# Who issues the weight loads: SyncE's queue or GpSimd's own, in a two-block transformer kernel

## The chip, the cores and the metric

The kernel runs on one core of one Trainium2 chip. The metric is the device time of one launch, in microseconds (us); lower is better. Everything is float32 in memory. The engines are TensorE (PE in the profile, its weight load PEld), VectorE (DVE), ScalarE (ACT), GpSimd (POOL) and SyncE (SP), which here computes nothing and only issues transfers.

## The reference

One sequence of 1024 tokens with 1024 features goes through two blocks.

```
first block:   mod = c @ w_ada + b_ada            -> shift, scale, gate (1024 each)
               h = rmsnorm(x) * (1 + scale) + shift
               proj = h @ w_in                    -> glu, z, q, k, v, gates
               y_conv = (silu(layernorm(conv31(glu))) * silu(z_conv)) @ w_conv_out
               y_att  = (3 groups of dilated window attention * silu(z_att)) @ w_att_out
               x = rmsnorm(x + gate * ((sig(g1) * y_conv + sig(g2) * y_att) @ w_o))
second block:  proj = rmsnorm(x) @ w_in2 + b      -> pool, q, k, v, gates
               merged = sig * (pooling @ w) + sig * (window attention @ w)
               x = x + rmsnorm(merged @ w_out2)
               x = x + rmsnorm(relu(rmsnorm(x) @ w_up)^2 @ w_down),  4096 hidden features
```

## The kernel before, in words

**Three products for one.** Each float32 operand of a large product is cut into a high half (rounded to TensorE's fast float32 form) and a low half (the rest). A product is then three passes: high by high, high by low, low by high. Activations are cut by ScalarE (`act_hi`) and VectorE (`act_lo`, line 1239). Weights are cut by GpSimd.

**Pieces, chunks, units.** The weights of the projections come in `PIECES` of 128 x 512 values (256 KB); eight make a chunk of 512 output columns. A piece is loaded into one of four buffers (`raw`, `RAW = 4`). GpSimd copies it to `w_hi` (line 870) and subtracts to get `w_lo` (line 872), in the helper `split_piece`; the semaphore `w_ready` counts the finished ones. `w_hi` and `w_lo` hold two chunks, so the cutting of chunk c begins (gate `acc_ready` in the loop over `PIECES`) when TensorE has ended chunk c - 2. TensorE works a chunk as units of 24 (or 12) matmuls into four PSUM banks. The names of the chunks that matter below: `q`, `k`, `v` of three attention groups; `za`, `zc` (gates); `yc`, `ya` (the two output projections of block one), `wo`; `pl`, `q3`, `kv3`, `g2p`, `g2a`, `yp`, `yb`, `w2` in block two; then 16 rounds of the MLP, each with four `up` and four `down` pieces.

**SyncE's order.** All transfers are issued by SyncE in one program order: `next_piece` (line 507) waits for `w_ready >= n - 3`, so that the buffer is free, and issues piece n; `prefetch(u)` calls it as the program passes unit u, between stores, activations' loads and other traffic. At the start SyncE issues x, the pieces of `w_ada` (`ada_piece`, line 537, eight buffers), stores four rows of `mod`, reads shift and scale back (lines 564 and 565), then calls `next_piece` eight times, and only then issues `w_ada` pieces 32 to 47, which are the `gate` rows. TensorE's program has all six `w_ada` rows (`ada_row_`, line 1777) ahead of the first projection. In the MLP SyncE's loop calls `mlp_pieces` (line 793).

**Stretches in which VectorE's work stands between two stretches of matmuls:**

- "h": affine (line 1291) and low half (line 1239) of the first activations.
- "Z": while `zc` is computed, each of eight token blocks is combined from three attention groups (lines 1429 to 1432), transposed, and loaded for the next (lines 669, 677).
- "uz": after `zc`, 8 rounds of lines 1456, 1457, 1459 and 1239 before `yc` can go on.
- "az", "mg" and "m2": low halves (line 1239) before `ya`, `wo` and `w2`.
- "q3": pooling (lines 1565 to 1570) and rotation in the `q3` chunk.
- "norm 2": lines 1502 to 1536 during `w2`, before the MLP.

Of the kernel before, what the change touches and what calls it, by code (L numbers as in the profile page):

```python
# [42 lines left out]
RAW = 4  # L43
# [134 lines left out]
def build(nc, A, out):  # L178

    chunks, units, items, U, chunk_last = plan()  # L180
# [9 lines left out]
    with ExitStack() as ctx:  # L190
# [213 lines left out]
        def unit_range(first, last):  # L404
            return units[U[first]:U[last] + 1]
# [87 lines left out]

        @block.sync
        def _(sp):
            piece = [0]

            def next_piece():

                n = piece[0]  # L500
                if n >= NP0:
                    return
                if n >= RAW:
                    sp.wait_ge(w_ready, n - RAW + 1)
                c, s = PIECES[n]
                for cols, src in piece_src(chunks[c], s):
                    sp.dma_start(raw[:, n % RAW, cols], src).then_inc(raw_ld[n % RAW], 16)
                piece[0] += 1

            def prefetch(u):  # L510

                if u in unit_chunk:
                    c, i = unit_chunk[u]
                    if i < 8 and piece[0] < 8 * (c + 1) + i + 1:
                        next_piece()

            def store_item(u, dst):
                wait_evac(sp, u)
                sp.dma_start(dst, slot(u)).then_inc(ev_st[E[u] % EVN], 16)
# [43 lines left out]
                sp.wait_ge(mod_st[n], v)  # L563
            sp.dma_start(c_sh, cols_of(mod_d[0, 0:D]), allow_slow_non_contiguous=True).then_inc(ada_col, 16)
            sp.dma_start(c_gs, cols_of(mod_d[0, D:2 * D]), allow_slow_non_contiguous=True).then_inc(ada_col, 16)
            for _ in range(8):
                next_piece()
            for p in range(32, 48):
                ada_piece(p)
            for n in (4, 5):  # L570
# [62 lines left out]
            def attention_io(g):  # L633
                per = att_share(len(ATT_STAGES[g]))
                us = att_units(g)
                for s in range(64):
                    for i in units_done(len(ATT_STAGES[g]), s):
                        u = us[i]
                        prefetch(u)
                        if i >= 1 and us[i - 1][0] in DST:  # L640
                            w = us[i - 1]
                            store_item(w, feature_tile(DST[w[0]], w[1], w[2]))
                        if i >= 1 and us[i - 1] == ("ua", 1, 1):
                            conv_load(0)
                            conv_load(1)
                    conv_io(("step", g, s))
                    if g < 3 and s >= 6 and (s - 6) % 4 == 1:
                        store_heads(g, s - 4)
                w = us[-1]
                store_item(w, feature_tile(DST[w[0]], w[1], w[2]))  # L650
                if g < 3:
                    store_heads(g, 63)
                    store_stats(g)

            def qkv_io(g):
                for u in STAGE_QKV[g]:
                    prefetch(u)
                    conv_io(u)

            for g in range(NG):  # L660
# [31 lines left out]
            attention_block(0)  # L692
            late = None
            for u in STAGE_Z:
                prefetch(u)
                if u[0] == "zc":
                    if late:
                        store_item(late, feature_tile(DST["zc"], late[1], late[2]))
                    late = u
                if u[0] == "lt" and u[2] == 1 and u[1] + 1 < NB:  # L700
                    conv_block(u[1] + 1)
                if u[0] == "at" and u[1] + 1 < NB:
                    attention_block(u[1] + 1)
# [20 lines left out]

            i = 0
            for u in units[U[("yc", 0, 0)]:U[("ya", 7, 1)] + 1]:
                prefetch(u)
                gate_load(i, ("uz", 7), u, "gc" if u[0] == "yc" else "ga")
                i += 1

# [11 lines left out]
            n = 0  # L742
            for h in range(2):
                for B in range(NB):
                    prefetch(("wo", B, h))
                    if n >= 2:
                        sp.wait_ge(n_x[0], n - 1)
                    sp.dma_start(xt2[n % 2], A["x"][0, P * B:P * B + P, HALF * h:HALF * h + HALF]
                                 ).then_inc(n_ld[0][n % 2], 16)
                    n += 1  # L750
                    if h and B >= 2:
                        sp.wait_ge(n_y[0], B - 1)
                        sp.dma_start(x1_d[P * (B - 2):P * (B - 1), :], tokT[:, B - 2, :]).then_inc(n_st[0], 16)
# [3 lines left out]


            b2 = A["b_in_2"]
            for u in unit_range(("pl", 0, 0), ("pl", 3, 1)):  # L760
                prefetch(u)
# [7 lines left out]
            for u in unit_range(("q", 3, 0), ("kt", 3, 7)):  # L769
                prefetch(u)  # L770
            for t in range(4):
                for h in range(2):
                    wait_evac(sp, ("pm", t, h))
# [7 lines left out]
                    for h in range(2):  # L781
                        wait_stored(sp, (n, t, h))
            for i, u in enumerate(unit_range(("yp", 0, 0), ("yb", 7, 1))):
                prefetch(u)
                gate_load(i + 32, ("y2", 3), u, "g2p" if u[0] == "yp" else "g2a")


            def mlp_pieces(src, j, before):

                for p in range(4):  # L790
                    sp.wait_ge(w_ready, before + p)
                    dst = raw[:, p, :].rearrange("p (k n) -> p k n", k=2) if src is up_src else raw[:, p, :]
                    sp.dma_start(dst, src(j, p)).then_inc(raw_ld[p], 16)
# [4 lines left out]
            sp.wait_ge(n_st[0], 16 * 8)  # L798
            for h in range(2):
                for B in range(NB):  # L800
                    prefetch(("w2", B, h))
                    if h:
                        if B >= 2:
                            sp.wait_ge(n_y[1], B - 1)
                        sp.dma_start(res[B % 2], x1_d[P * B:P * B + P, :]).then_inc(n_ld[1][B % 2], 16)
                        if B >= 2:
                            sp.dma_start(x2_d[P * (B - 2):P * (B - 1), :], tokT[:, B - 2, :]).then_inc(n_st[1], 16)
                        if B == 3:
                            mlp_pieces(up_src, 0, NP0 - 3)
            for B in (6, 7):  # L810
                sp.wait_ge(n_y[1], B + 1)
                sp.dma_start(x2_d[P * B:P * B + P, :], tokT[:, B, :]).then_inc(n_st[1], 16)


            with sp.Fori(1, NJ) as k:
                mlp_pieces(up_src, k, NP0 + 8 * k - 7)
                mlp_pieces(down_src, k - 1, NP0 + 8 * k - 3)
            mlp_pieces(down_src, NJ - 1, NP0 + 8 * NJ - 7)


            sp.wait_ge(n_xn[1], 8)
# [17 lines left out]
        def _(pool):  # L839
# [25 lines left out]

            pool.iota(posi[:, 24:32], pattern=[[P, 8]], base=0, channel_multiplier=1).then_inc(consts, 1)

            def split_piece(n, src, dhi, dlo):

                pool.tensor_copy(dhi, src).then_inc(w_hi_done, 1)  # L870
                pool.wait_ge(w_hi_done, n + 1)
                pool.tensor_tensor(dlo, src, dhi.bitcast(F32), ALU.subtract).then_inc(w_ready, 1)  # L872

            for n, (c, s) in enumerate(PIECES):
                pool.wait_ge(raw_ld[n % RAW], raw_total[n])
                if c >= 2 and s == 0:
                    pool.wait_ge(acc_ready, U[chunk_last[c - 2]] + 1)
                split_piece(n, raw[:, n % RAW, :], w_hi[:, c % 2, s, :], w_lo[:, c % 2, s, :])
                if chunks[c] == ("kv", 3) and s == 7:

                    pool.wait_ge(att_max, 64 * NG)
                    pool.affine_select(out=band[:, :], in_=band[:, :], compare_op=ALU.is_gt, fill=NEG, base=0,
                                       pattern=[[1, 2 * P]], channel_multiplier=-1).then_inc(consts, 1)

            def mlp_split(region, n0, ld, free):

                pool.wait_ge(acc_ready, free)
                for p in range(4):
                    pool.wait_ge(raw_ld[p], RAW_BASE[p] + 16 * (ld + 1))
                    pool.sem_inc(piece_seen)  # L890
                    split_piece(n0 + p, raw[:, p, :], w_hi[:, 0, region + p, :], w_lo[:, 0, region + p, :])


            last_chunk = len(chunks) - 1
            mlp_split(0, NP0, 0, U[chunk_last[last_chunk - 1]] + 1)
            mlp_split(4, NP0 + 4, 1, U[chunk_last[last_chunk - 1]] + 1)
            mlp_split(0, NP0 + 8, 2, M0 + 4)
            with pool.Fori(2, NJ) as k:

                mlp_split(4, NP0 + 8 * k - 4, 2 * k - 1, M0 + 20 * k - 32)  # L900
                mlp_split(0, NP0 + 8 * k, 2 * k, M0 + 20 * k - 16)
            mlp_split(4, NP0 + 8 * NJ - 4, 2 * NJ - 1, M0 + 20 * NJ - 32)

            for B in range(NB):
                pool.wait_ge(n_scaled, B + 1)
# [1068 lines left out]
```

## Time and profile before

| | |
|---|---|
| median of 3 runs | 2915.23 us (2912.63 to 2915.69) |
| profiled execution, its own time | 2915.05 us |
| its span, first to last instruction | 2912.9 us |
| mean granted TensorE clock | 0.971 of full |
| busy: TensorE, VectorE, GpSimd, ScalarE | 95%, 48%, 31%, 22% of the span |

The profile is one execution. A view lists either groups of instructions by source line, or the instructions in order of time (start, duration, engine, line, operation, output and input tile), with the idle time before one and what ended it in square brackets. "SPq" rows are issues by SyncE's queue; their duration is from the first to the last issue of the row. Two views give the waits: one by who waited for whom, one (the chain) that follows the work that ended last back to its start.

### The profile page before, as it was taken

The numbers are of one execution on the slowest core, as the hardware profiler recorded it, in microseconds if no ns is written. First come the engines' busy times: TensorE is split into PE (matmuls) and PEld (weight loads), VectorE is DVE, ScalarE is ACT, GpSimd is POOL, SyncE is SP. The second block draws the span as 40 slices with busy tenths as digits, with TensorE's granted clock in tenths as the row PEclk, the third lists the DMA queues.
The fourth block names the chain that finished last, engine by engine and source line by source line (L and its number), as shares of the span: only waits on it lengthen the run. The fifth ranks groups of instructions, "written<-read, shape, count | busy, mean of one in ns | idle before, by whom it ended". The sixth has DMA issues, their size and how long they took to land.

```text
span 2912.9 us, 33971 instructions
## 1 busy us (share of the span) xinstructions
PE 2759.7 (95%) x12436; PEld 2198.0 (75%) x12436; DVE 1386.1 (48%) x2569; ACT 627.4 (22%) x1495; POOL 897.2 (31%) x870
## 2 busy tenths in 40 slices
PE   6799999999999999877999989998999999999997
PEld 2487778987789877765778767776787888888886
DVE  1421245986667676564346432223545344344346
ACT  3212222112321122441014022222122101101102
POOL 0531122432224232222424322222323343343343
PEclk8899999999999999997999989999999999999999
DMA  5410111122212132453334122223422111111113
GB/s 174 131 51 26 57 55 58 56 66 75 84 54 73 49 98 84 158 165 122 100 111 148 30 67 65 59 65 127 130 94 98 44 50 50 43 51 50 43 54 126
DMA packets 155596, 236.10 MB, mean 81 GB/s; under 512 B 24764, under 2 KB 69564, under 8 KB 155464
## 3 DMA queue, kind: packets, MB, share of 16 engines
q1 hardware_dynamic: 155464, 234.35, 25.3%
q8 instruction: 82, 1.34, 0.2%
q14 instruction: 50, 0.41, 0.0%
HBM read 181.65 MB, written 52.64 MB: 80 GB/s over the span
## 4 chain that ended last, share of the span: by engine, by line
PE 87%; DVE 8%; DMA 3%; ACT 1%; issue 1%; POOL 0%; SPq 0%; POOLq 0%; ACTq 0%; DVEq 0%
PE ps L1748 50%; PE ps L1895 12%; PE ps L1927 11%; PE ps L1806 5%; PE ps L1816 3%; PE ps L1830 3%; PE ps L1760 2%; PE ps L1777 2%; DVE act_lo L1239 1%; DVE scr L1326 1%; DMA small<-st_d 1%; DMA scr<-in_x 1%; DVE scr L1429 0%; DVE big L1669 0%; DVE big L1519 0%
## 5 line engine op out<-in xcount | busy, mean ns | idle before, releaser
L870 POOL CAST w_hi<-raw 128x512 fp32r<-128x512 f32 x416 | 306.0, 736 | 1948.5 <-DMA raw<-in_w_in 938.3
L1748 PE MATMUL ps<-act_hi,w_hi 128*128 128x512 f32 x1344 | 557.6, 415 | 48.4 <-DVE act_lo L1239 46.2
L872 POOL TENSOR_TENSOR w_lo<-raw,w_hi 128x512 fp32r<-128x512 f32 x416 | 580.3, 1395 | 33.3
L1748 PE MATMUL ps<-act_lo,w_hi 128*128 128x512 f32 x1344 | 532.6, 396 | 0.0
L1748 PE MATMUL ps<-act_hi,w_lo 128*128 128x512 f32 x1344 | 530.2, 394 | 0.0
L1326 DVE SCALAR_TENSOR_TENSOR scr<-scr,small 128x512 f32<-128x512 f32 x480 | 421.0, 877 | 11.5
L1748 PE MATMUL ps<-w_hi,act_hi 128*128 128x512 f32 (+1 forms) x960 | 387.4, 404 | 6.8 <-DVE act_lo L1239 6.5
L1748 PE MATMUL ps<-w_hi,act_lo 128*128 128x512 f32 (+1 forms) x960 | 376.0, 392 | 0.0
L1748 PE MATMUL ps<-w_lo,act_hi 128*128 128x512 f32 (+1 forms) x960 | 375.8, 391 | 0.0
L1748 PEld LDWEIGHTS ps<-act_hi,w_hi 128*128 128x128 f32 x1344 | 256.4, 191 | 102.2 <-issue 54.3
L1748 PEld LDWEIGHTS ps<-act_lo,w_hi 128*128 128x128 f32 x1344 | 255.6, 190 | 57.6
L1748 PEld LDWEIGHTS ps<-act_hi,w_lo 128*128 128x128 f32 x1344 | 257.0, 191 | 45.7 <-issue 0.2
L1748 PEld LDWEIGHTS ps<-w_hi,act_hi 128*128 128x128 f32 x960 | 233.3, 243 | 31.8 <-issue 12.5
L1748 PEld LDWEIGHTS ps<-w_hi,act_lo 128*128 128x128 f32 x960 | 233.5, 243 | 21.0
L1748 PEld LDWEIGHTS ps<-w_lo,act_hi 128*128 128x128 f32 x960 | 234.4, 244 | 19.1
L1018 ACT ACTIVATE scr<-scr,stat 128x256 f32<-128x256 f32 (+1 forms) x256 | 118.6, 463 | 512.6 <-DVE stat L1349 511.2
L1681 DVE TENSOR_TENSOR big<-big,ps 128x512 f32<-128x512 f32 x224 | 150.0, 684 | 112.5 <-PE ps L1927 112.5
L1895 PE MATMUL ps<-act_hi,w_hi 128*128 128x512 f32 x512 | 200.1, 391 | 1.8 <-DVE act_lo L1536 1.8
L1895 PE MATMUL ps<-act_lo,w_hi 128*128 128x512 f32 x512 | 199.9, 390 | 0.0
L1895 PE MATMUL ps<-act_hi,w_lo 128*128 128x512 f32 x512 | 199.8, 390 | 0.0
L1927 PE MATMUL ps<-w_hi 128*128 128x512 f32 x512 | 199.3, 389 | 0.0
L1927 PE MATMUL ps<-w_lo,w_hi 128*128 128x512 f32 x512 | 199.2, 389 | 0.0
(173 smaller groups left out, 3113.5 us busy)
## 6 DMA issues: line engine op xcount, KB each, us to landing
raw<-in_w_in SPq DMA_DIRECT2D x176, 256.0 KB, 3.1
raw<-in_w_up SPq DMA_DIRECT2D x64, 256.0 KB, 2.7
raw<-in_w_down SPq DMA_DIRECT2D x64, 256.0 KB, 2.6
vreg<-in_w_ada SPq DMA_DIRECT2D x48, 256.0 KB, 3.5
raw<-in_w_in SPq DMA_DIRECT2D x72, 128.0 KB, 2.2
x_d<-big SPq DMA_DIRECT2D x16, 512.0 KB, 3.0
scr<-x_d SPq DMA_DIRECT2D x16, 512.0 KB, 4.2
o_d<-scr SPq DMA_DIRECT2D x48, 128.0 KB, 1.9
```

The costliest lines, as they stand in the source:

```text
L870: pool.tensor_copy(dhi, src).then_inc(w_hi_done, 1)
L872: pool.tensor_tensor(dlo, src, dhi.bitcast(F32), ALU.subtract).then_inc(w_ready, 1)
L1018: nc.scalar.activation(prob[a % 2][:, 0:n], prob[a % 2][:, 0:n], ACT.Exp, scale=-1.0, bias=stat[:, B, h:h + 1], accum_out=stat[:, B, 8 + h ...
L1326: nc.vector.scalar_tensor_tensor(ca, u_in[:, j:j + HALF], w[:, j:j + 1], ca, ALU.mult, ALU.add).then_inc(tap, 1)
L1681: ins = nc.vector.tensor_tensor(dst, dst, acc[i % ACC], ALU.add)
L1748: ins = nc.tensor.matmul(out_, lhs, rhs, start=(m == 0), stop=(m == 3 * nk - 1))
L1760: ins = nc.tensor.transpose(bank(u)[:, P * i:P * i + P], src, ident[:, :])
L1806: nc.tensor.matmul(ps_s[a % 2][:, 0:n], qT[rows, pair, P * B:P * B + P], keys, start=True, stop=True).then_inc(scores, 1)
L1816: ins = nc.tensor.transpose(ps_t[:, P * i:P * i + P], prob[a % 2][:, P * i:P * i + P], ident[:, :])
L1830: ins = nc.tensor.matmul(ps_o[:, 0:HD], probT[a % 2][:, P * i:P * i + P], v, start=(i == 0), stop=(i == n // P - 1))
L1895: ins = nc.tensor.matmul(out_, up_w[b][:, k, P * t:P * t + P], act_p[a][:, k, HALF * h:HALF * h + HALF], start=(m == 0), stop=(m == 23))
L1927: ins = nc.tensor.matmul(acc[i % ACC], hid[a][:, par, k, P * B:P * B + P], down_w[b][:, k, HALF * h:HALF * h + HALF], start=(m == 0), stop ...
```

## The change

GpSimd issues every weight piece itself. It starts the first four before its loop. After it has cut piece n it waits until its own low half is written (`w_ready >= n + 1`) and issues piece n + 4 into the buffer just read. The MLP's pieces follow in the same way from `mlp_split`, whose last argument says what to load. SyncE loses `next_piece`, `prefetch`, `mlp_pieces` and its MLP loop; all its other transfers stay in their order, with nothing between them.

```diff
@@ block.sync
-            def next_piece():
-                n = piece[0]
-                if n >= RAW:
-                    sp.wait_ge(w_ready, n - RAW + 1)
-                c, s = PIECES[n]
-                for cols, src in piece_src(chunks[c], s):
-                    sp.dma_start(raw[:, n % RAW, cols], src).then_inc(raw_ld[n % RAW], 16)
-            def prefetch(u): ...
@@ between the loads of shift and scale and w_ada pieces 32 to 47
-            for _ in range(8):
-                next_piece()
             for p in range(32, 48):
                 ada_piece(p)
...
-            with sp.Fori(1, NJ) as k:
-                mlp_pieces(up_src, k, NP0 + 8 * k - 7)
-                mlp_pieces(down_src, k - 1, NP0 + 8 * k - 3)
-            mlp_pieces(down_src, NJ - 1, NP0 + 8 * NJ - 7)
@@ block.gpsimd
+            def mlp_load(src, j, p):
+                dst = raw[:, p, :].rearrange("p (k n) -> p k n", k=2) if src is up_src else raw[:, p, :]
+                pool.dma_start(dst, src(j, p)).then_inc(raw_ld[p], 16)
+            def load_piece(n):
+                if n >= NP0:
+                    mlp_load(up_src, 0, n - NP0)
+                    return
+                c, s = PIECES[n]
+                for cols, src in piece_src(chunks[c], s):
+                    pool.dma_start(raw[:, n % RAW, cols], src).then_inc(raw_ld[n % RAW], 16)
             def split_piece(n, src, dhi, dlo):
                 pool.tensor_copy(dhi, src).then_inc(w_hi_done, 1)
                 pool.wait_ge(w_hi_done, n + 1)
                 pool.tensor_tensor(dlo, src, dhi.bitcast(F32), ALU.subtract).then_inc(w_ready, 1)
+                pool.wait_ge(w_ready, n + 1)
+            for n in range(RAW):
+                load_piece(n)
             for n, (c, s) in enumerate(PIECES):
                 pool.wait_ge(raw_ld[n % RAW], raw_total[n])
                 if c >= 2 and s == 0:
                     pool.wait_ge(acc_ready, U[chunk_last[c - 2]] + 1)
                 split_piece(n, raw[:, n % RAW, :], w_hi[:, c % 2, s, :], w_lo[:, c % 2, s, :])
+                load_piece(n + RAW)
...
-            def mlp_split(region, n0, ld, free):
+            def mlp_split(region, n0, ld, free, after):
                 pool.wait_ge(acc_ready, free)
                 for p in range(4):
                     pool.wait_ge(raw_ld[p], RAW_BASE[p] + 16 * (ld + 1))
                     pool.sem_inc(piece_seen)
                     split_piece(n0 + p, raw[:, p, :], w_hi[:, 0, region + p, :], w_lo[:, 0, region + p, :])
+                    if after:
+                        mlp_load(after[0], after[1], p)
...
-                mlp_split(4, NP0 + 8 * k - 4, 2 * k - 1, M0 + 20 * k - 32)
-                mlp_split(0, NP0 + 8 * k, 2 * k, M0 + 20 * k - 16)
+                mlp_split(4, NP0 + 8 * k - 4, 2 * k - 1, M0 + 20 * k - 32, (down_src, k - 1))
+                mlp_split(0, NP0 + 8 * k, 2 * k, M0 + 20 * k - 16, (up_src, k + 1))
```

## Rows read from the trace of the kernel before

**Rows 1.** The page's chain of work that ended last, by engine.

```profile
PE 87%; DVE 8%; DMA 3%; ACT 1%; issue 1%; POOL 0%; SPq 0%; POOLq 0%; ACTq 0%; DVEq 0%
```

**Rows 2.** TensorE's waits: total us, times, longest.

```profile
PE ps L1777 <- DMA vreg<-in_w_ada: 20.6, 1, 20.6
```

**Rows 3.** Order of time, SyncE's queue, 72 to 112 us: start, duration.

```profile
74.11 15.46 SPq L507 DMA_DIRECT2D raw<-in_w_in  x8
89.62 12.70 SPq L537 DMA_DIRECT2D vreg<-in_w_ada  x16
```

**Rows 4.** Order of time, TensorE, 75 to 112 us.

```profile
92.80 9.16 PE L1777 MATMUL ps<-vreg,small 128*1 128x512 f32 x16 [20.59 <-DMA vreg<-in_w_ada]
...
109.79 0.50 PE L1748 MATMUL ps<-w_hi,act_hi 128*128 128x512 f32 x1
```

**Rows 5.** Groups of VectorE by line, 76 to 101.6 us: busy us, mean ns.

```profile
L1239 DVE TENSOR_TENSOR act_lo<-big,act_hi 128x1024 fp32r<-128x1024 f32 x8 | 17.4, 2182 | 0.1
```

**Rows 6.** Order of time, VectorE, 0 to 62 us.

```profile
7.41 0.75 DVE L1245 TENSOR_SCALAR scr<-scr,small 128x1024 f32<-128x1024 f32 x1
```

**Rows 7.** Windows, first 12 us: busy, clock, DMA share, GB/s.

```profile
0.00:12.00 12.00, 3.63 (x16) 3.28 (x16) 1.84 (x4) 6.54 (x10) 3.80 (x29) 1.00 0.80 274
```

**Rows 8.** All instructions on the buffers `raw`: ns minimum, median, maximum.

```profile
L870 POOL CAST w_hi<-raw x416: 601/613/3265, 77.2 to 2860.1; 128x512 fp32r<-128x512 f32 x139
L872 POOL TENSOR_TENSOR w_lo<-raw,w_hi x416: 1261/1292/2152, 78.0 to 2860.8; 128x512 fp32r<-128x512 f32 x139
...
L793 SPq DMA_DIRECT2D raw<-in_w_down x64: 327/336/346, 2208.9 to 2839.7; - x64
```

**Rows 9.** Order of time, VectorE, "uz": first operation and last ones.

```profile
1305.36 0.81 DVE L1456 TENSOR_SCALAR big<-big,col 128x1024 f32<-128x1024 f32 x1 [7.25 <-ACT scr L1080]
...
1331.34 1.22 DVE L1457 SCALAR_TENSOR_TENSOR big<-scr,big 128x1024 f32<-128x1024 f32 x1
...
1334.88 1.10 DVE L1456 TENSOR_SCALAR big<-big,col 128x1024 f32<-128x1024 f32 x1
1336.01 2.18 DVE L1457 SCALAR_TENSOR_TENSOR big<-scr,big 128x1024 f32<-128x1024 f32 x1
```

**Rows 10.** Order of time, VectorE, "Z".

```profile
1190.60 1.90 DVE L1429 TENSOR_TENSOR scr<-scr,stat 128x512 f32<-128x512 f32 x3
...
1205.92 3.41 DVE L1429 TENSOR_TENSOR scr<-scr,stat 128x512 f32<-128x512 f32 x3
...
1295.93 1.28 DVE L1338 SCALAR_TENSOR_TENSOR scr<-scr,ps 128x512 f32<-128x512 f32 x2
```

**Rows 11.** Order of time, TensorE, "Z".

```profile
1211.88 1.50 PE L1760 MATMUL ps<-ident,scr 128*128 128x128 f32 x12 [1.12 <-DVE scr L1338]
...
1294.07 0.39 PE L1748 MATMUL ps<-act_lo,w_hi 128*128 128x512 f32 x1
```

**Rows 12.** Order of time, VectorE, "az" and "mg".

```profile
1427.73 7.36 DVE L1239 TENSOR_TENSOR act_lo<-vreg,act_hi 128x1024 fp32r<-128x1024 f32 x4 [0.40 <-ACT act_hi L922]
...
1479.93 9.16 DVE L1239 TENSOR_TENSOR act_lo<-big,act_hi 128x1024 fp32r<-128x1024 f32 x8
```

**Rows 13.** Order of time, GpSimd, the end of "m2".

```profile
2100.48 3.27 POOL L870 CAST w_hi<-raw 128x512 fp32r<-128x512 f32 x1 [33.47 <-DMA raw<-in_w_out]
```

**Rows 14.** Order of time, VectorE, "q3".

```profile
1669.14 0.69 DVE L1581 TENSOR_TENSOR scr<-ps,big 128x512 f32<-128x512 f32 x1 [3.06 <-PE ps L1748]
...
1689.25 0.17 DVE L1309 TENSOR_TENSOR scr<-scr 128x16 f32<-128x16 f32 x1
```

**Rows 15.** Order of time, VectorE, "norm 2": the same line two blocks apart.

```profile
2164.22 1.28 DVE L1514 SCALAR_TENSOR_TENSOR big<-big,stat,vreg 128x1024 f32<-128x1024 f32 x1
...
2179.58 1.28 DVE L1514 SCALAR_TENSOR_TENSOR big<-big,stat,vreg 128x1024 f32<-128x1024 f32 x1
...
2193.34 1.28 DVE L1514 SCALAR_TENSOR_TENSOR big<-big,stat,vreg 128x1024 f32<-128x1024 f32 x1
```

**Rows 16.** The chain in order of time, MLP: half of a round.

```profile
2331.08 21.76 PE ps L1927 x96
```

More of the change, by code:

```diff
@@ L495, in _ @@
         def _(sp):
-            piece = [0]
-            def next_piece():
-                n = piece[0]
-                if n >= NP0:
-                    return
-                if n >= RAW:
-                    sp.wait_ge(w_ready, n - RAW + 1)
-                c, s = PIECES[n]
-                for cols, src in piece_src(chunks[c], s):
-                    sp.dma_start(raw[:, n % RAW, cols], src).then_inc(raw_ld[n % RAW], 16)
[L508 to L514, printed above, removed]
-                        next_piece()
             def store_item(u, dst):
@@ L565, in _ @@
             sp.dma_start(c_gs, cols_of(mod_d[0, D:2 * D]), allow_slow_non_contiguous=True).then_inc(ada_col, 16)
-            for _ in range(8):
-                next_piece()
             for p in range(32, 48):
@@ L638, in attention_io @@
                         u = us[i]
-                        prefetch(u)
                         if i >= 1 and us[i - 1][0] in DST:
@@ L656, in qkv_io @@
                 for u in STAGE_QKV[g]:
-                    prefetch(u)
                     conv_io(u)
@@ L694, in _ @@
             for u in STAGE_Z:
-                prefetch(u)
                 if u[0] == "zc":
@@ L726, in _ @@
             for u in units[U[("yc", 0, 0)]:U[("ya", 7, 1)] + 1]:
-                prefetch(u)
                 gate_load(i, ("uz", 7), u, "gc" if u[0] == "yc" else "ga")
@@ L744, in _ @@
                 for B in range(NB):
-                    prefetch(("wo", B, h))
                     if n >= 2:
@@ L759, in _ @@
             b2 = A["b_in_2"]
-            for u in unit_range(("pl", 0, 0), ("pl", 3, 1)):
-                prefetch(u)
             sp.wait_ge(n_st[0], 16 * 8)
@@ L768, in _ @@
             sp.dma_start(wpool, A["w_pool_2"][0].rearrange("g c d -> c g d")).then_inc(p_in, 16)
-            for u in unit_range(("q", 3, 0), ("kt", 3, 7)):
-                prefetch(u)
             for t in range(4):
@@ L783, in _ @@
             for i, u in enumerate(unit_range(("yp", 0, 0), ("yb", 7, 1))):
-                prefetch(u)
                 gate_load(i + 32, ("y2", 3), u, "g2p" if u[0] == "yp" else "g2a")
[L788 to L793, printed above, removed]
             wait_evac(sp, ("yb", 7, 1))
@@ L800, in _ @@
                 for B in range(NB):
-                    prefetch(("w2", B, h))
                     if h:
@@ L807, in _ @@
                             sp.dma_start(x2_d[P * (B - 2):P * (B - 1), :], tokT[:, B - 2, :]).then_inc(n_st[1], 16)
-                        if B == 3:
-                            mlp_pieces(up_src, 0, NP0 - 3)
             for B in (6, 7):
@@ L891, in mlp_split @@
                     split_piece(n0 + p, raw[:, p, :], w_hi[:, 0, region + p, :], w_lo[:, 0, region + p, :])
+                    if after:
+                        mlp_load(after[0], after[1], p)
             last_chunk = len(chunks) - 1
[L895 to L898, printed above, removed]
-                mlp_split(4, NP0 + 8 * k - 4, 2 * k - 1, M0 + 20 * k - 32)
-                mlp_split(0, NP0 + 8 * k, 2 * k, M0 + 20 * k - 16)
-            mlp_split(4, NP0 + 8 * NJ - 4, 2 * NJ - 1, M0 + 20 * NJ - 32)
+            mlp_split(0, NP0, 0, U[chunk_last[last_chunk - 1]] + 1, (up_src, 1))
+            mlp_split(4, NP0 + 4, 1, U[chunk_last[last_chunk - 1]] + 1, (down_src, 0))
+            mlp_split(0, NP0 + 8, 2, M0 + 4, (up_src, 2))
+            with pool.Fori(2, NJ - 1) as k:
+                mlp_split(4, NP0 + 8 * k - 4, 2 * k - 1, M0 + 20 * k - 32, (down_src, k - 1))
+                mlp_split(0, NP0 + 8 * k, 2 * k, M0 + 20 * k - 16, (up_src, k + 1))
+            k = NJ - 1
+            mlp_split(4, NP0 + 8 * k - 4, 2 * k - 1, M0 + 20 * k - 32, (down_src, k - 1))
+            mlp_split(0, NP0 + 8 * k, 2 * k, M0 + 20 * k - 16, (down_src, NJ - 1))
+            mlp_split(4, NP0 + 8 * NJ - 4, 2 * NJ - 1, M0 + 20 * NJ - 32, None)
             for B in range(NB):
```

## The prediction

> **What bounds the kernel now.** I read four views in this order. The chain of work that ended last first: TensorE holds 87% of it and VectorE 8%; GpSimd and SyncE's queue hold next to nothing [rows 1]. So a change of who issues the weights can pay only where TensorE stands still. Then TensorE's waits: it never waits for a weight piece, but once, for 20.6 us, for a piece of `w_ada` [rows 2]. Then the order of time around that wait: SyncE spends 74.11 to 89.57 us in its eight `next_piece` calls, each held by GpSimd's cutting, and the 16 `w_ada` pieces go out only behind them, at 89.62 [rows 3]. TensorE, which ended its fourth row at 92.80 - 20.59 = 72.2 us, starts the fifth at 92.80 and the first projection at 109.79 [rows 4]. Last, the stretches where VectorE is on the chain, to see what GpSimd does beside them, because the change moves GpSimd's work in time.
>
> **Part 1, the start.** Without the eight calls the `w_ada` pieces go out at 74.11, so rows five and six and the first projection come 89.62 - 74.11 = 15.5 us earlier, at about 94.3. What would be late next is "h". VectorE's low halves there took 2.18 us each [rows 5] beside GpSimd's cutting; alone they take 9.16 / 8 = 1.145 [rows 12] and the affine 0.75 [rows 6]. GpSimd is through with both chunks by then, so "h" takes 8 x 1.9 = 15.2 us from 76.6 and ends near 92, under 94.3: the whole 15.5 counts. Against it: GpSimd now works at 6 to 60 us, beside the x stage, in which each pair of token blocks is load, square, scale, transpose, next load. In the first 12 us the DMA engines are 80% busy at 274 GB/s [rows 7], so some 342 GB/s is full. Four pieces (1 MB, 3.1 us) fall into that; half of it ahead of the x loads is 1.5 us, later pairs 0.5 together. The scaling (0.75) becomes some 1.1 when GpSimd is busy, as line 1456 of the same shape did [rows 9]: 3 x 0.35 = 1.0. Cost 3.0, between 0 and 8 (both fully serial). Part 1: **-12.5**, from -15.5 to -7.5.
>
> **The price of one issue on GpSimd.** No row has it. The nearest is SyncE's issue of the same piece, 0.34 us [rows 8]; the other end is the whole path of a transfer, 92.80 - 89.62 = 3.2 us from issue to use [rows 3, 4]. I take 1.0: the two are far apart, and it lies nearer to the issue row, between GpSimd's two operations on a piece, 0.61 and 1.29 [rows 8]. A piece then holds GpSimd 1.9 + 1.0 = 2.9 us, and the eight of a chunk some 23 us of a chunk's 48 to 77, so TensorE still never waits for weights. In the MLP a half round is 21.76 us of TensorE [rows 16] and four pieces are 11.6.
>
> **The price of a piece to VectorE.** At the end of "uz" one piece came beside lines 1456 and 1457: 1.10 and 2.18 us instead of 0.75 [rows 6] and 1.22 [rows 9], so 1.3 us for each piece. The Trainium skill (SBUF — State Buffer, Who interferes with whom) says that a VectorE operation with two inputs in SBUF and a GpSimd operation that reads SBUF exclude each other for a whole instruction. By that a piece would cost VectorE up to GpSimd's full 1.9 us, and the three stretches of part 2 that get worse would cost half as much again; the row, with 1.3, is what I use.
>
> **Part 2, where the cutting moves.** Before, SyncE's program order spread a chunk's loads over the stretch; now four pieces lie ready and the other four come fast, so all eight are cut in one burst as soon as the gate of chunk c - 2 opens. The stretches, each with its gate:
>
> "Z". Each block's combination ran beside two pieces: 3.41 us instead of 1.90 on line 1429 alone [rows 10], and TensorE waited 1.1 us in every second block [rows 11]. The burst of `zc` 1 starts with the end of `za`, 17 us before the first combination [rows 10], and is over 23 us later; that of `yc` 0 starts at half time and takes two blocks. Two of the waits go (-2.2). At the end, 1295.93 + 1.28 = 1297.2 [rows 10] can't come earlier than TensorE's last matmul, 1294.46 [rows 11], plus 0.6: -2.1. **-4.3**, from -6 to 0.
>
> "uz". The gate of `yc` 1 opens at 1294.46. VectorE's "uz" starts at 1305.36 [rows 9], 2.1 less after "Z", so 8.8 us behind the gate (3.0 pieces at 2.9), and 5.0 pieces fall into it: 6.5 us, less the 1.3 of the one that is there now. **+5.0**, from +1 (the issue delays GpSimd, not VectorE) to +9.
>
> "mg" and "m2". Before, the eight low halves ran undisturbed, 1.145 each [rows 12], because the next piece landed only at their end; now the burst starts with them. Two rows disagree on what that does. In "az", where the burst starts together with them, an operation took 7.36 / 4 = 1.84 [rows 12]. In "m2" a copy of GpSimd that arrived in the middle of the row of low halves waited 2.7 of its 3.27 us until they were over [rows 13]: VectorE lost nothing. After its first piece GpSimd now stops for an issue and comes back in the middle; so I take the second row behind a first collision of 1.3 and something more, 2.0 for each. **+4.0**, from +2.6 to +14 (0.7 x 8 and the collision, twice). "az" stays.
>
> "q3". The burst is there before and after, at the same gate: eight pieces, 1669.14 to 1689.4 [rows 14], in which VectorE lost 8 x 1.3 of its 20.3 us. With 1.0 for the issue the pieces come 3.5 us apart instead of 2.5, VectorE works at 1 - 1.3 / 3.5 = 0.63, and its 9.9 us of work take 15.7: -4.6; I take **-4.0**, from -5 to 0 (the issue blocks VectorE's small copies as well).
>
> "norm 2". Four pieces of `up` 0 fell into it: two blocks took 2179.58 - 2164.22 = 15.36 us, two undisturbed ones 13.76 [rows 15], so 0.4 for each piece, because much of this chain is ScalarE's. Now the gate, the end of `w2` 0 at the stretch's beginning, lets eight pieces run there. **+1.6**, up to 8 x 1.3 - 1.6 = +8.8.
>
> Everything else (attention; the two 2 MB transfers beside attention 3; the rounds of the MLP; SyncE's other transfers, which only come sooner) hides under TensorE: **+1.0** for small losses, 0 to +4. If the cover in attention were gone, nine chunks' bursts would cost VectorE's 8 x 1.3 = 10 us each; the chain [rows 1] says it is there, with 8% for all of VectorE.
>
> **The sum.** -12.5 - 4.3 + 5.0 + 4.0 - 4.0 + 1.6 + 1.0 = -9.2 us. It is made against the profiled execution's own 2915.05 us (span 2912.9 and 2.15 around it), which lies 0.2 us from the median of 2915.23: 2905.9, so **2906 us**.
>
> **Rivals.** (a) The bursts cost nothing: VectorE keeps its turn as in "m2", and only the start moves. Then -12.5 - 4.3 + 1.0 = -15.8: 2899. For it: [rows 13]. Against: [rows 9, 12].
>
> (b) The start's gain is mostly eaten, by the x stage (8 instead of 3) and by seven pieces in "uz" (7.8 instead of 5.0): -9.2 + 5 + 2.8 = -1.4, so 2914, no difference that can be told. For it: 80% DMA share in the first 12 us [rows 7]. To it I count that the change doesn't do what it says, because TensorE's fifth row then waits for something else; nothing in [rows 3, 4] points to that.
>
> (c) Slower, one mechanism: GpSimd and VectorE take turns at every operation wherever a burst meets a row of low halves or norms, as in "az". "mg" and "m2" then cost 13.8 instead of 4.0, "norm 2" 8.8 instead of 1.6, "q3" gains nothing: -9.2 + 9.8 + 7.2 + 4.0 = +11.8, so 2927. It decides the sign once these stretches lose 9 us more than I give them.
>
> (d) Slower by far: the issue on GpSimd is long. A round of the MLP has eight pieces in 43.5 us [rows 16]; from 43.5 / 8 - 1.9 = 3.5 us for an issue on, GpSimd bounds it. At 4.0 that is 8 x 5.9 - 43.5 = 3.7 us in 15 rounds, 56 us: 2960. It takes more than the upper bound above.
>
> The Trainium skill (SBUF — State Buffer, SBUF: two separate sides) warns that descriptors of a transfer issued by GpSimd are written by its cores through the port that VectorE's two-port operations lock. By that the transfers, not VectorE, would be late, by at most one such operation of 0.75 us each: hidden behind four buffers, no term of the sum. No trace of before shows it.
>
> **Chances.** The forecast 0.42 (its own range 2900 to 2909), (a) 0.14, (b) 0.27, (c) 0.12, (d) 0.05. About 0.2%, 5.8 us, is what a measurement of this kernel can tell from no change. Faster by more (below 2909.4): the forecast and (a), 0.56. Within: (b), 0.27. Slower: (c) and (d), 0.17. The range takes in (a) and its lower edge, (b), and the lower part of (c): 2894 to 2923.
>
> **What would show it.** Fifth `w_ada` row near 80 us (77.3 plus 3 from the x stage) and first projection near 97, with `w_hi` copies starting near 10 us. Low halves of "h" near 1.15 us. In "uz" some five GpSimd pieces and about 39 us instead of 35. In "mg" low halves that together take 11 us or less; 15 would be (c). GpSimd 2.9 us between two copies of a burst; near 5.5 would be (d), with matmuls of the MLP waiting for `w_lo`. Wrong at once: a fifth row later than 85 us, or MLP rounds longer than 43.5.

## The result, and the profile after

The changed kernel takes **2938.2 us** (median of 4 runs, 2937.7 to 2943.2) against 2915.2 for the kernel before: a ratio of 1.0085, 95% interval 1.0067 to 1.0102. It is slower by 23 us, where 2906 was predicted. The profiled execution has a span of 2935.7 us, 22.8 longer than that of before.

The page of the changed kernel, busy times and the chain by engine, beside [rows 1]:

```profile
PE 2773.6 (94%) x12436; PEld 2203.6 (75%) x12436; DVE 1423.0 (48%) x2569; ACT 626.9 (21%) x1495; POOL 1137.2 (39%) x1318
...
PE 85%; DVE 10%; DMA 2%; ACT 1%; issue 1%; POOLq 0%; POOL 0%; SPq 0%; ACTq 0%; DVEq 0%
```

VectorE's share of the chain has grown from 8% to 10% of the span; GpSimd still holds none of it. GpSimd has 448 more instructions, which are its issues. TensorE's waits (total us, times, longest), beside [rows 2]:

```profile
PE ps L1721 <- DVE act_lo L1212: 67.8, 24, 22.3
...
PE ps L1733 <- DVE scr L1282: 16.5, 7, 6.5
...
PE ps L1750 <- DMA vreg<-in_w_ada: 5.2, 1, 5.2
```

The wait for `w_ada` fell from 20.6 to 5.2 us. The wait for low halves rose from 52.7 to 67.8. The wait for the rotation (line 1282; line 1309 before) is 16.5 us in seven waits where it was 15.8 in five; most of both is in "q3".

TensorE in order of time, the fifth `w_ada` row and the first projection, beside [rows 4]:

```profile
80.92 8.69 PE L1750 MATMUL ps<-vreg,small 128*1 128x512 f32 x16 [5.16 <-DMA vreg<-in_w_ada]
...
97.45 0.50 PE L1721 MATMUL ps<-w_hi,act_hi 128*128 128x512 f32 x1
```

The start came as forecast: 97.4 instead of 109.8, 12.4 us earlier. All of it, and 23 us more, is lost behind it. The table gives how far the changed kernel is behind the kernel before at the same instruction of both traces, and what each stretch added:

| reached | us behind | stretch added | predicted |
|---|---|---|---|
| first projection | -12.4 | -12.4 | -12.5 |
| second attention (qkv of group 1 inside) | -5.1 | +7.3 | |
| start of "Z" | -4.1 | +1.0 | |
| end of "Z", start of "uz" | +0.4 | +4.5 | -4.3 |
| end of "uz" | +5.8 | +5.4 | +5.0 |
| "az" and `ya` over | +5.1 | -0.7 | |
| "mg" over | +10.5 | +5.4 | +2.0 |
| "q3" over | +6.7 | -3.8 | -4.0 |
| `kv3` and pooling over | +9.8 | +3.1 | |
| attention 3 over | +10.6 | +0.8 | |
| gated sums of block two over | +13.9 | +3.3 | |
| "m2" over | +20.9 | +7.0 | +2.0 |
| "norm 2" over, MLP starts | +21.3 | +0.4 | +1.6 |
| end | +22.8 | +1.5 | |

The stretches with an empty last column are "everything else": 7.3 + 1.0 - 0.7 + 3.1 + 0.8 + 3.3 + 1.5 = 16.3 us, for which the prediction had 1.0. The end of "Z" is VectorE's last operation there; TensorE's last matmul of `zc` is 1.8 us behind, and "uz" starts 1.7 behind. The start of one execution can be 4 us off that of another with the same instructions up to there (see the last section), so differences between stretches are more reliable than the first line.

"mg" in order of time, GpSimd of the changed kernel:

```profile
1483.24 0.60 POOL L834 CAST w_hi<-raw 128x512 fp32r<-128x512 f32 x1 [25.02 <-PE ps L1721]
1483.93 1.74 POOL L836 TENSOR_TENSOR w_lo<-raw,w_hi 128x512 fp32r<-128x512 f32 x1
1485.97 0.56 POOL L830 DMA_DIRECT2D raw<-in_w_o  x1 [0.30 <-POOL w_lo L836]
1486.53 0.69 POOL L834 CAST w_hi<-raw 128x512 fp32r<-128x512 f32 x1
1487.31 2.13 POOL L836 TENSOR_TENSOR w_lo<-raw,w_hi 128x512 fp32r<-128x512 f32 x1
1489.74 0.56 POOL L830 DMA_DIRECT2D raw<-in_w_o  x1 [0.30 <-POOL w_lo L836]
```

and VectorE beside it, the row of [rows 12]:

```profile
1484.47 15.14 DVE L1212 TENSOR_TENSOR act_lo<-big,act_hi 128x1024 fp32r<-128x1024 f32 x8
```

Three readings. The gate opens 1.2 us ahead of the row, so the burst and the eight low halves start together. The period of a piece is 1489.74 - 1485.97 = 3.77 us, in which VectorE does two low halves of 1.145: a piece costs VectorE 3.77 - 2.29 = 1.5 us, and the row 15.14 - 9.16 = 6.0 us for four pieces. And the issue on GpSimd is short: 0.56 us, with 0.30 of waiting for its own low half ahead of it. The MLP's half round stayed at 21.76 us.

Two of the eight low halves by themselves, the first beside a cast, the second beside a subtraction:

```profile
1486.68 1.63 DVE L1212 TENSOR_TENSOR act_lo<-big,act_hi 128x1024 fp32r<-128x1024 f32 x1
1488.23 2.30 DVE L1212 TENSOR_TENSOR act_lo<-big,act_hi 128x1024 fp32r<-128x1024 f32 x1
```

An undisturbed one shows 1.22 us (0.08 of it overlaps with the next). So the cast costs VectorE 0.41 of its 0.60 us, the subtraction 1.08 of its 1.27, and the two add up to the 1.5.

"m2" is the same row once more, 15.14 us instead of 9.16. Another 1.0 us is lost there behind the row: TensorE's granted clock is 0.69 in the 22 us from 2106, against 0.91 before in the 18 us from 2092, and until 2125.1 us a matmul takes 0.63 us instead of 0.39.

"Z": the burst of `yc` 0 opens at 1234.74 and its later pieces meet the combination of one block. VectorE of the changed kernel, where lines 1402, 1404 and 1405 are lines 1429, 1431 and 1432 of before:

```profile
1245.84 3.72 DVE L1402 TENSOR_TENSOR scr<-scr,stat 128x512 f32<-128x512 f32 x3
1249.59 1.46 DVE L1404 TENSOR_TENSOR scr<-scr 128x512 f32<-128x512 f32 x1
1251.08 1.64 DVE L1405 TENSOR_TENSOR scr<-scr 128x512 f32<-128x512 f32 x1
```

In the blocks that no piece meets these take 1.90 [rows 10], 0.69 and 0.69. TensorE then waited 5.3 us in one go, where the kernel before had waits of 1.1 in every second block [rows 11]. In the runs `mid_row` and `qkv1_paced` below, whose cuts in "Z" are those of the changed kernel, this one wait is 6.2 us.

Queries and keys of group 1: VectorE in order of time, five filter taps (line 1299) behind the rotation, beside the burst of `v` 1:

```profile
514.35 8.18 DVE L1299 SCALAR_TENSOR_TENSOR scr<-scr,small 128x512 f32<-128x512 f32 x5
...
525.19 5.28 DVE L1299 SCALAR_TENSOR_TENSOR scr<-scr,small 128x512 f32<-128x512 f32 x5
```

and five taps of the kernel before (line 1326) that no piece meets:

```profile
532.84 3.90 DVE L1326 SCALAR_TENSOR_TENSOR scr<-scr,small 128x512 f32<-128x512 f32 x5
```

TensorE's wait for the rotation in this stretch, before (471 to 700 us) and after (459 to 700):

```profile
PE ps L1760 <- DVE scr L1309: 1.5, 1, 1.5
```

```profile
PE ps L1733 <- DVE scr L1282: 4.2, 3, 2.2
```

What the prediction should have read here is a row of windows of the kernel before (us, then busy us of TensorE, its weight load, VectorE, ScalarE and GpSimd):

```profile
523.00:550.00 27.00, 25.51 (x116) 24.98 (x116) 24.60 (x45) 4.46 (x8) 4.69 (x5) 1.00 0.09 27
```

VectorE is busy 24.60 of 27 us there. It has 2.4 us to spare in a unit group, and eight pieces in a burst ask for more.

The row "end" has another cause. It lies behind the last matmul, where GpSimd's program closes with a DRAIN, and every engine's last instruction comes after it. Before, and in the changed kernel (ns):

```profile
L190 POOLq DRAIN  x1: 2449/2449/2449, 2907.5 to 2907.5; - x1
```

```profile
L190 POOLq DRAIN  x1: 6633/6633/6633, 2928.8 to 2928.8; - x1
```

From the last matmul to the end of the span it is 15.9 us in the kernel before and in each of the runs below in which GpSimd issues nothing, and 17.3 or 17.4 in each in which GpSimd issues the pieces. These 1.5 us are a fixed price of the issuer, not of the bursts.

### The profile page after: what moved, and what is told of

Read it like the earlier page. It is cut to its first block, busy times and chain, and to the rows that moved or that the text cites. A ratio compares the mean times of both kernels' runs of the same rounds, so it can differ in the third digit from the quotient of the medians.

```text
span 2935.7 us, 33773 instructions
## 1 busy us (share of the span) xinstructions
PE 2773.6 (94%) x12436; PEld 2203.6 (75%) x12436; DVE 1423.0 (48%) x2569; ACT 626.9 (21%) x1495; POOL 1137.2 (39%) x1318
## 4 chain that ended last, share of the span: by engine, by line
PE 85%; DVE 10%; DMA 2%; ACT 1%; issue 1%; POOLq 0%; POOL 0%; SPq 0%; ACTq 0%; DVEq 0%
PE ps L1721 49%; PE ps L1868 12%; PE ps L1900 11%; PE ps L1779 5%; PE ps L1789 3%; DVE scr L1299 3%; PE ps L1803 3%; PE ps L1733 2%; DVE act_lo L1212 2%; PE ps L1750 2%; DMA scr<-in_x 1%; DVE big L1430 0%; DVE big L1642 0%; DVE big L1492 0%; DVE big L1432 0%
## 5 line engine op out<-in xcount | busy, mean ns | idle before, releaser
L834 POOL CAST w_hi<-raw 128x512 fp32r<-128x512 f32 x416 | 271.1, 652 | 1558.3 <-PE ps L1721 1239.3
L1299 DVE SCALAR_TENSOR_TENSOR scr<-scr,small 128x512 f32<-128x512 f32 x480 | 450.0, 938 | 11.5
L1721 PE MATMUL ps<-w_hi,act_hi 128*128 128x512 f32 (+1 forms) x960 | 389.9, 406 | 13.9 <-DVE act_lo L1212 13.9
```

What stands on the lines that cost most here:

```text
L1299: nc.vector.scalar_tensor_tensor(ca, u_in[:, j:j + HALF], w[:, j:j + 1], ca, ALU.mult, ALU.add).then_inc(tap, 1)
L1721: ins = nc.tensor.matmul(out_, lhs, rhs, start=(m == 0), stop=(m == 3 * nk - 1))
```

## The experiments

The explanation to be tested: the loss comes from *when* GpSimd cuts, in bursts, and not from *who* issues. Each run is timed against the kernel before; the intervals are of 95%.

### 1. The start alone

```diff
+            for _ in range(4):
+                next_piece()
             def mod_store(n):
...
-            for _ in range(8):
-                next_piece()
-            for p in range(32, 48):
+            for p in range(32, 40):
+                ada_piece(p)
+            for _ in range(4):
+                next_piece()
+            for p in range(40, 48):
                 ada_piece(p)
```

> The kernel before, SyncE keeps every transfer; only the order of its queue at the start is changed (four pieces ahead of the first store of mod_d, then c_sh and c_gs, eight w_ada pieces, four pieces, eight w_ada pieces). Theory (the changed kernel loses by its bursts of cutting, and the start's gain has nothing to do with who issues): the first projection comes 15 us earlier than before and nothing is given back behind it, 2900 us, with low halves of mg at 9.1 us and m2 at 9.1. Rival (an earlier start is given back downstream whatever the cutting does, because the stretches are bound by something that doesn't move): 2908 to 2915.

Measured: **2899.65 us**, ratio 0.9945 (0.9931 to 0.9959). As was expected, nothing is given back from the first projection (-14.3) to the end (-14.4), and the low halves of "mg" and "m2" take 9.16 and 9.17 us. The start's gain needs no other issuer, only another order in SyncE's queue.

### 2. GpSimd issues, but the cuts are paced

In the changed kernel, the cut of piece s of a chunk waits for a unit of the chunk before.

```diff
                 if c >= 2 and s == 0:
                     pool.wait_ge(acc_ready, U[chunk_last[c - 2]] + 1)
+                if c >= 1 and s >= 1:
+                    pool.wait_ge(acc_ready, U[UNIT_AT[c - 1, s - 1]] + 1)
```

> The changed kernel, GpSimd issues, but the cut of piece s of a chunk waits for unit s - 1 of the chunk before, the pace that SyncE's program order gave in the kernel before. Theory (bursts): start -12.4 as in the changed kernel, low halves of mg back at 9 to 10 us from 15.1 and of m2 from 13.5, Z and the first attention stretches as before, q3 without its gain of 3.8; about 2903 us, between 2900 and 2908. Rival (the issue on GpSimd, or the queue that its transfers take, is what costs): 2930 or more, the losses stay where they are.

Measured: **2895.21 us**, 0.9931 (0.9917 to 0.9945), 43 us less than the changed kernel for one line of waiting, and 8 below the 2903 that were expected. Its VectorE row in "m2", which one piece meets:

```profile
2071.62 10.24 DVE L1215 TENSOR_TENSOR act_lo<-big,act_hi 128x1024 fp32r<-128x1024 f32 x8
```

"mg" has the same 10.24. Queries and keys give nothing back. Two things differ from the expectation. From "mg" to the end of pooling it is 5.7 us faster than before (-13.8 to -19.5), where a loss against the changed kernel was expected: the kernel before bursts there too, and the pace takes that away. "Z" still loses 4.7 us (-14.8 at its start, -10.1 at its end; see experiment 6), "m2" 1.1 to its one piece, and the DRAIN at the end 1.4.

### 3. SyncE issues, but half of the cuts come in a burst

Order as in `start_only`, and a look-ahead of four more pieces:

```diff
-                    if i < 8 and piece[0] < 8 * (c + 1) + i + 1:
+                    if i < 8 and piece[0] < 8 * (c + 1) + i + 5:
```

> SyncE issues everything, start order as in start_only, but the look-ahead of the weight pieces is four larger, so four of a chunk's eight pieces lie in the buffers when the gate opens and are cut in one burst, the other four at the pace of the units. Half of the changed kernel's burst, with no issue on GpSimd. Theory (bursts): loses about half of the 35 us that the changed kernel gives back behind its start, or somewhat less as the first pieces of a burst are the ones that collide: 2908 to 2918 us, low halves of mg 11 to 13 us. Rival (issue or queue costs, not the burst): the same as start_only, 2900, low halves of mg 9.1.

Measured: **2930.05 us**, 1.0051 (1.0037 to 1.0064), more than expected because of a slip of the edit: eight pieces stood behind the 40th of `w_ada` in SyncE's queue and held the last eight back. SyncE's queue of this run in order of time:

```profile
74.24 3.89 SPq L537 DMA_DIRECT2D vreg<-in_w_ada  x8
78.18 20.25 SPq L507 DMA_DIRECT2D raw<-in_w_in  x8
98.47 3.75 SPq L537 DMA_DIRECT2D vreg<-in_w_ada  x8
```

so the start's gain was missing (+0.1 at the first stores of `u`). The same run with four pieces ahead of the last eight of `w_ada` and four behind:

> start_ahead4 with the order of the start mended: its eight pieces behind the 40th w_ada piece held the last eight w_ada pieces back, so that it had none of the start's gain; now four go ahead of these and four behind. SyncE issues everything, four of a chunk's pieces are cut in a burst. Theory (start and bursts add up): 14.3 us less than start_ahead4, 2915 to 2917, so the half bursts alone cost 15 to 17 us against start_only. Rival (what start_ahead4 lost is of the start's order, not of the bursts): 2900 to 2905.

Measured: **2914.96 us**, 1.0006 (0.9997 to 1.0015), 15.1 less. Start and bursts add up: half bursts, with SyncE as the issuer, cost 15.3 us against `start_only`. (The trace of this run starts unusually early, -19.2 at the first projection, and gives back 19.3.) The first of the two runs shows "mg" with the changed kernel's price, although GpSimd issues nothing. VectorE:

```profile
1481.04 15.16 DVE L1244 TENSOR_TENSOR act_lo<-big,act_hi 128x1024 fp32r<-128x1024 f32 x8
```

and GpSimd:

```profile
1482.20 1.60 POOL L875 CAST w_hi<-raw 128x512 fp32r<-128x512 f32 x1
1483.88 2.14 POOL L877 TENSOR_TENSOR w_lo<-raw,w_hi 128x512 fp32r<-128x512 f32 x1
1485.97 1.60 POOL L875 CAST w_hi<-raw 128x512 fp32r<-128x512 f32 x1
```

The period is 1485.97 - 1482.20 = 3.77 us again. Where the changed kernel has a wait and an issue (0.86) and then a cast of 0.69, this one has a cast of 1.60, which waits for VectorE's operation. The issue's time lies inside the turn that VectorE has anyway.

### 4. A burst that arrives in the middle of the row

The prediction had taken the late cast of [rows 13] as its rule: a row that is going keeps VectorE's turn.

```diff
+                if s == 0 and chunks[c] in (("wo", 1), ("w2", 1)):
+                    pool.wait_ge(lo_done, SPLIT_LO[("mg" if chunks[c][0] == "wo" else "m2", 2)])
```

> The changed kernel, but the burst that meets the low halves of mg, and the one that meets those of m2, start when the third low half of the row is done, not together with the row. Theory (who is first decides: a copy of GpSimd that arrives in the middle of a running row waits until the row is over, as one did in m2 of the kernel before): the rows take 9.2 to 9.5 us instead of 15.1, GpSimd's first cast there is 5 to 6 us long, and the kernel is 6.0 + 4.4 = 10.4 us faster than the changed one: 2928. Rival (they take turns wherever a burst meets a row): five low halves are left, two to three pieces of 1.5 us, the rows take 12 to 13.5, 2933 to 2935.

Measured: **2934.02 us**, 1.0070 (1.0057 to 1.0082): the rival's number. GpSimd and, in the second fence, VectorE in "mg":

```profile
1490.07 1.44 POOL L834 CAST w_hi<-raw 128x512 fp32r<-128x512 f32 x1 [29.71 <-DVE act_lo L1214]
1491.60 2.15 POOL L836 TENSOR_TENSOR w_lo<-raw,w_hi 128x512 fp32r<-128x512 f32 x1
1494.04 0.56 POOL L830 DMA_DIRECT2D raw<-in_w_o  x1 [0.30 <-POOL w_lo L836]
```

```profile
1486.42 12.18 DVE L1214 TENSOR_TENSOR act_lo<-big,act_hi 128x1024 fp32r<-128x1024 f32 x8
```

The cast waits for one low half and no more, and two pieces cost the row 12.18 - 9.16 = 3.0 us, 1.5 each. That arriving first decides is refuted as a rule. Why the casts of [rows 13] and of `start_only` at the same place (3.55 us) did wait until the row was over stays open. It was no rule to build on.

### 5. Pacing in one stretch alone

Only `k` 1, `v` 1 and `glu` 3 of the changed kernel are paced, with the lines of experiment 2 under `chunks[c] in (("k", 1), ("v", 1), ("glu", 3))`.

> The changed kernel, but the pieces of the three chunks whose bursts fall into qkv of head group 1 (k 1, v 1, glu 3) are cut one per unit of the chunk before. Theory (the 7.3 us that the changed kernel gives back between 460 and 825 us come from the burst beside the five filter taps and the rotation, where VectorE is nearly full): these 7.3 us return and nothing else moves, 2931, and the store of the last u_d tile comes 12 to 13 us earlier than before instead of 5. Rival (they come from somewhere else, such as the later transfers of SyncE or the issue on GpSimd): within 2 us of the changed kernel, 2936 to 2940.

Measured: **2930.79 us**, 1.0062 (1.0050 to 1.0074), 7.4 less than the changed kernel, as the theory had it. The store of the last tile of `u` is 12.6 us ahead of before instead of 5.2, and TensorE's wait for the rotation is gone from the stretch. This is the largest part of the missed 16.3.

### 6. The same pace, SyncE as issuer

`start_only` with the two lines of experiment 2.

> SyncE issues every transfer, in the order of start_only, and GpSimd cuts at the pace of paced (the cut of piece s waits for unit s - 1 of the chunk before). The only difference to paced is who issues. Theory (the issuer does not matter, the time of the cuts does): within 3 us of paced, with the start 1.3 us better, 2892 to 2898. Rival (a part of the gain of paced over start_only, 4.5 us, is from the queue of GpSimd, whose transfers are there earlier): like start_only, 2900.

Measured: **2887.29 us**, 0.9907 (0.9894 to 0.9920), the fastest of all, 27.6 us or 0.9% below the kernel before. It is 8 us below `paced`, where at most 3 were expected, so it does matter who issues, by less than when one cuts. "Z" is where the stretches of the two traces differ most: it gives back 0.6 us here and 4.7 there. All loads from `st_d` in "Z", for `paced`:

```profile
L654 SPq DMA_DIRECT2D small<-st_d x7: 489/490/1594, 1185.5 to 1273.8; - x7
...
  DVE stat L1388: 26.2, 7
DMA to landing us min/median/max: 5.1/5.5/5.7
```

and for `sync_paced`:

```profile
L684 SPq DMA_DIRECT2D small<-st_d x7: 489/489/1760, 1182.6 to 1266.6; - x7
...
  DVE stat L1420: 19.5, 7
DMA to landing us min/median/max: 4.2/4.4/4.8
```

A block of "Z" waits for this small load. It lands 1.1 us later when a weight piece travels at the same time in a queue of its own, and VectorE waits 6.7 us more over seven blocks. In one queue the piece stands behind the block's loads: SyncE issues it 1.1 us or more after the small load, where GpSimd issues it at the same time or up to 1.1 us ahead. The Trainium skill (DMA: Bandwidth & Descriptors, Queues, rings and completion order) says that each DMA engine goes round-robin between the queues for which it has work. These two rows agree with it, but they do not tell the second queue from the earlier issue.

### 7. GpSimd pays the issue, the pieces stay with SyncE

To `sync_paced` a small transfer (128 rows of 64 bytes, to a buffer that nothing reads) is added behind each cut of the projections.

```diff
                 split_piece(n, raw[:, n % RAW, :], w_hi[:, c % 2, s, :], w_lo[:, c % 2, s, :])
+                pool.wait_ge(w_ready, n + 1)
+                pool.dma_start(dum_d[n], A["x"][0, 0:P, 0:16]).then_inc(dum_st, 16)
```

> sync_paced, plus one small transfer (128 rows of 64 bytes, 8 KB, from x to a buffer in memory that nothing reads) that GpSimd issues behind the low half of each piece of the projections. GpSimd pays its issue and the wait ahead of it as in paced, 0.86 us for each piece, but the 256 KB still travel in SyncE's queue. Theory (the 8 us between paced and sync_paced come from the pieces' transfers, which in a queue of their own run beside the loads of a block in Z and slow them, small from st_d 5.6 us to landing instead of 4.4): as sync_paced, 2887 to 2889. Rival (the issue's own time on GpSimd, or what it does to VectorE, is the cost): 2893 to 2896.

Measured: **2894.06 us**, 0.9935 (0.9921 to 0.9948), the rival's number, while the profile speaks for the theory in its place: in "Z" the loads from `st_d` land after 4.3 us, VectorE waits 19.0 us for them, and the stretch gives back 1.2 us. The trace of this run is 4.4 us longer than that of `sync_paced`: 2.1 of it up to the last matmul (1.2 are there at the first projection) and 2.3 behind it, where GpSimd's DRAIN takes 7.5 us instead of 2.4.

Between the traces of `paced` and `sync_paced`, which are 6.1 us apart (8 in the medians), "Z" makes 4.1, the start 2.6, the DRAIN 1.4, and the stretches behind "Z" take 2.1 back. The DRAIN is shown. The slower load in "Z" is shown too, its price less firmly: `start_ahead4` and `ahead4_mended` run the same program in "Z" and lose 3.0 and 0 us there. The 2.6 of the start are within what starts differ by themselves (last section).

### 8. A tuned version with GpSimd as issuer

`paced`, with the first loads behind the x stage, `zc` 1 in one burst, `yc` 0 in pairs, and the first MLP pieces late:

```diff
+            pool.wait_ge(acc_ready, U[("xt", 7, 1)] + 1)
             for n in range(RAW):
                 load_piece(n)
...
+                if chunks[c] == ("yc", 0):
+                    pool.wait_ge(ln_rs, 5 + s // 2)
+                elif c >= 1 and s >= 1 and chunks[c] != ("zc", 1):
+                    pool.wait_ge(acc_ready, U[UNIT_AT[c - 1, s - 1]] + 1)
...
+            pool.wait_ge(n_y[1], 3)
             mlp_split(0, NP0, 0, ...)
```

> paced with four edits, GpSimd issues: the first loads wait for the end of the x stage; zc 1 is cut in one burst, ahead of the first combination; the pieces of yc 0 go two by two, each pair behind the layer norm's scale of a block, where VectorE then idles 3.3 us; the first MLP pieces wait until three blocks of norm 2 are done. Theory (a piece costs nothing where VectorE idles): start 1.3, Z 3 to 5, norm 2 3 us better than paced, 2886 to 2889. Rival (pairs of pieces reach into the combination, as in paced, and the later MLP pieces make TensorE wait): 2894 to 2898.

Measured: **2890.14 us**, 0.9917 (0.9903 to 0.9930), between the two numbers expected. Start (-14.6 against -13.0) and "Z" (4.7 lost becomes 0.7 gained: -14.7 at its start, -15.4 at its end) did what they should. The MLP's pieces did not: "norm 2" loses 1.8 us, where it lost 0.3 in `paced`, because all eight pieces now fall into its later half and meet VectorE's operations there. From -25.1 at the end of the gated sums it is -22.3 in the MLP, with 1.1 more lost in "m2". A version without that loss was not tried.

## Why the prediction was wrong, point by point

**The start** (-12.5) was right: -12.4. The fifth row came at 80.92 (forecast near 80), the first projection at 97.4 (near 97), and the low halves of "h" took 1.22 us.

**The issue on GpSimd** (1.0 us) was 0.56, with 0.30 of waiting ahead of it. The rival of a long issue is out. That it hides was right for the MLP. What it costs at the program's end, 1.5 us, was no term of the sum.

**The price of a piece** (1.3 us) was nearly right: 1.5 in a row of low halves. By the rule of the Trainium skill (SBUF — State Buffer, Who interferes with whom) it would be up to the full 1.9. The measured 1.5 decides: VectorE and GpSimd do take turns, but some 0.2 us of the cast and 0.2 of the subtraction cost VectorE nothing.

**"mg" and "m2"** (2.0 each) failed. They cost 5.4 and 7.0. The rows of low halves are 6.0 in each; in "m2" the lower clock adds 1.0, and ahead of "mg" 0.5 came back. The wrong step is "After its first piece GpSimd now stops for an issue and comes back in the middle; so I take the second row": [rows 13] was taken as the rule and "az" of [rows 12] as the exception. It is the other way round. The row of experiment 4 shows pieces that come back in the middle and wait for one low half at most, and experiment 3 shows the price without any issue. In this the rival of turns at every operation was right.

**"Z"** (-4.3) had the wrong sign: +4.5. The two-piece waits did go, but the burst of `yc` 0 was said to take two blocks and was given no price of its own; it met one combination at full density, lines 1402 to 1405, and held TensorE for 5.3 us. That the burst is all of it is not shown: `paced` loses as much in "Z" with its cuts spread, there beside the slower loads of experiment 6.

**"uz"** (+5.0) came out at +5.4, partly by luck. Only four pieces fell into it, not five, at 5.4 / 4 = 1.3 each less the one that was there before: 4.1 us. The other 1.3 are from its start, which follows TensorE's last matmul of `zc` (+1.8) and not VectorE's end of "Z", as the prediction had it. **"q3"** (-4.0) was right, at -3.8: there both kernels burst beside VectorE, and the issues between the pieces let VectorE through.

**"norm 2"** (+1.6) was +0.4, less than forecast.

**Everything else** (+1.0) was 16.3, the largest miss. The step that failed is "the chain says it is there, with 8% for all of VectorE". The chain told that VectorE did not bound those stretches at the *old* spread of the cuts; how much slack it had per unit, 2.4 of 27 us in the queries and keys of group 1, stands only in the windows. The text itself had named the price, 10 us for a chunk whose cover is gone. Experiment 5 shows the burst as the cause for 7.4 us of it. The 3.1 us at `kv3` and pooling go away with the pace too (experiment 2). The 3.3 us in the gated sums are not settled: the load of the pooled tile took 9.3 us there instead of 7.8, and no run isolates it. The last 1.5 us are the DRAIN.

**The sum.** 15.3 (everything else) + 8.8 ("Z") + 8.4 ("mg", "m2") - 0.5 (start, "uz", "q3", "norm 2" together) = 32.0, and -9.2 + 32.0 = 22.8 us, the difference of the spans. The rival on the slower side, (c), gave 2927. Its mechanism was the right one, and its 13.8 us for "mg" and "m2" are close to the 12.4 measured. For "norm 2" (8.8) and "q3" (nothing gained) it was wrong, and its list of places was too short.

## What to carry to other kernels

When a load is moved to the engine that consumes it, the transfers' old program order goes with it, and that order may have been the pacing of the work behind them: ask what spread the work before, and put the spread back as a wait on the producer's progress (one line, worth 43 us here). Read slack from windows of one unit's length, with the neighbour engine's busy time beside it; a share of the chain says what binds at today's spacing, not what will bind if the same work comes in a burst. And test a gain apart from the vehicle that brings it: the 14 us of the start were a matter of order in SyncE's queue, and the fastest version keeps SyncE as the issuer.

## What the runs showed of the hardware that was not expected

- Two-input operations of VectorE (low half, 128 x 1024) and GpSimd's cast and subtraction (128 x 512) take strict turns: 3.77 us for two low halves and one piece, whether GpSimd issues in between or not. The cast costs VectorE 0.41 us, the subtraction 1.08.
- A single cast of GpSimd can still be kept waiting until the end of such a row (3.27 us in [rows 13], 3.55 in `start_only`); in `mid_row` one of the same kind waited for one operation only. What decides was not found.
- An issue by GpSimd takes 0.56 us for a piece of 128 rows of 2 KB, 0.72 for an `up` piece; SyncE's takes 0.34 [rows 8].
- GpSimd's closing DRAIN takes 6.6 us in every kernel in which it issued the weight pieces (7.5 in `sync_paced_small`) and 2.4 in every kernel in which it issued nothing; the stretch from the last matmul to the end is 1.4 to 2.3 us longer there.
- The same instructions can start differently: TensorE's fifth `w_ada` row began at 78.60 us in `start_only` and 74.19 in `ahead4_mended`, whose queues are the same up to there.
